# A bias moved into a matrix product, and two attention chunks contracted in halves

## What is computed

```python
x = layer_norm(ALPHA * x + mix, ln_mix_g[i], ln_mix_b[i])
x = layer_norm(ALPHA * x + swiglu(x, w_ffn_gate[i], w_ffn_up[i], w_ffn_down[i]), ln_ffn_g[i], ln_ffn_b[i])
gate = sigmoid(x @ w_ple_gate[i] + b_ple_gate[i])
x = x + (p[i] @ w_ple[i]) * gate          # then layer 1: qkv = x @ w_qkv + b_qkv, and attention
```

## Time and profile before

| | us |
|---|---|
| median of 3 runs | 1343.62 (1341.12 to 1346.0) |
| the profiled execution | 1346.43 |
| its span in the trace | 1344.5 |
| PE busy in the span | 1290.2 (96%) |
| DVE, ACT, POOL busy | 416.1, 648.8, 947.8 |
| mean granted clock of PE | 0.988 |

### The profile page before, as it was taken

One profiled execution on the slowest core, in us unless ns is written; L12 is line 12 of the kernel. 1 busy time (PEld: TensorE's weight loads), 2 busy tenths in 40 slices (PEclk: granted clock), 3 DMA queues, 4 the chain that ended last, 5 costly groups with the idle time before them and its releaser, 6 DMA issues.

```text
span 1344.5 us, 19614 instructions
## 1 busy us (share of the span) xinstructions
PE 1290.2 (96%) x8203; PEld 1154.0 (86%) x8203; DVE 416.1 (31%) x755; ACT 648.8 (48%) x841; POOL 947.8 (70%) x416
## 2 busy tenths in 40 slices
PE   6999999999999999999999999999988878999997
PEld 6988988878899988897899889998878658999885
DVE  5526325442222210045552131101153452101124
ACT  5673545755455553343444454435356544443442
POOL 6864246846969888756478778879976346786983
PEclk9999999999999999998999999999999998999999
DMA  8744134534656555635355756646637334663651
GB/s 276 210 128 126 48 110 132 182 108 127 220 152 199 183 195 195 188 93 159 104 173 188 245 169 183 175 138 211 224 113 265 108 94 129 172 193 119 234 189 47
DMA packets 117966, 218.60 MB, mean 163 GB/s; under 512 B 9415, under 2 KB 18934, under 8 KB 117750
## 3 DMA queue, kind: packets, MB, share of 16 engines
q1 hardware_dynamic: 113888, 209.92, 50.6%
q10 hardware_dynamic: 3990, 7.42, 1.6%
HBM read 216.27 MB, written 1.05 MB: 162 GB/s over the span
## 4 chain that ended last, share of the span: by engine, by line
PE 89%; DVE 7%; ACT 2%; issue 1%; DMA 1%; ACTq 0%; DVEq 0%
PE acc L1868 13%; PE acc L1870 13%; PE acc L1871 13%; PE acc L1861 12%; PE acc L1863 12%; PE acc L1862 12%; PE pm L1876 8%; PE acc L1819 1%; PE acc L1820 1%; PE acc L1821 1%; ACT pm L548 1%; PE pm L1785 1%; DMA ct<-in_consts 1%; DVE XTlo L1063 0%; DVE pm L1734 0%
## 5 line engine op out<-in xcount | busy, mean ns | idle before, releaser
L533 POOL TENSOR_TENSOR wlo<-raw,whi 128x1024 fp32r<-128x1024 f32 (+2 forms) x412 | 947.6, 2325 | 382.1 <-ACT whi L548 380.6
L548 ACT ACTIVATE whi<-raw 128x1024 fp32r<-128x1024 f32 (+2 forms) x412 | 412.4, 1019 | 354.1 <-PE acc L1871 154.2
L1868 PE MATMUL acc<-XThi,whi 128*128 128x256 f32 x1424 | 406.8, 286 | 5.5 <-issue 2.9
L1870 PE MATMUL acc<-XTlo,whi 128*128 128x256 f32 x1424 | 405.3, 285 | 0.0
L1871 PE MATMUL acc<-XThi,wlo 128*128 128x256 f32 x1424 | 405.3, 285 | 0.0
L1868 PEld LDWEIGHTS acc<-XThi,whi 128*128 128x128 f32 x1424 | 275.8, 194 | 6.9 <-issue 3.7
L1870 PEld LDWEIGHTS acc<-XTlo,whi 128*128 128x128 f32 x1424 | 275.8, 194 | 0.2
L1871 PEld LDWEIGHTS acc<-XThi,wlo 128*128 128x128 f32 x1424 | 275.7, 194 | 0.0
L1861 PE MATMUL acc<-whi,XThi 128*128 128x512 f32 (+3 forms) x320 | 125.8, 393 | 2.6 <-DVE xbcT L1492 1.6
L1863 PE MATMUL acc<-whi,XTlo 128*128 128x512 f32 (+3 forms) x320 | 121.5, 380 | 0.0
L1862 PE MATMUL acc<-wlo,XThi 128*128 128x512 f32 (+3 forms) x320 | 121.5, 380 | 0.0
(11 more groups left out here) (405 smaller groups left out, 1657.7 us busy)
## 6 DMA issues: line engine op xcount, KB each, us to landing
raw<-in_w_in SPq DMA_DIRECT2D x68, 512.0 KB, 3.7
raw<-in_w_ff SPq DMA_DIRECT2D x64, 512.0 KB, 3.7
raw<-in_w_in_mix SPq DMA_DIRECT2D x44, 512.0 KB, 3.6
raw<-in_w_down SPq DMA_DIRECT2D x44, 512.0 KB, 4.3
raw<-in_w_gate SPq DMA_DIRECT2D x40, 512.0 KB, 3.6
raw<-in_w_up SPq DMA_DIRECT2D x40, 512.0 KB, 3.7
raw<-in_w_branch SPq DMA_DIRECT2D x16, 512.0 KB, 3.5
raw<-in_w_out_mix SPq DMA_DIRECT2D x16, 512.0 KB, 3.5
```

Source lines behind the costliest of these rows:

```text
L533: nc.gpsimd.tensor_tensor(wlo[:, u % SPLIT, 0:nk, 0:width], raw[:, u % RAW, 0:nk, 0:width], whi[:, u % SPLIT, 0:nk, 0:width].bitcast(F32), ...
L548: return nc.scalar.activation(out_, in_, func, **k)
L1868: T.matmul(o, wh[:, fs], hi[:, k, :], start=opens and f % 2 == 0, stop=False, skip_group_check=True)
L1870: T.matmul(o, wh[:, fs], lo[:, k, :], start=False, stop=False, skip_group_check=True)
```

## The change

Two edits. First, `aq0` and `ak` are each cut into two chunks of 4 blocks: `aq0a`, `aka`, `aq0`, `ak` in this order, the first two `PARTIAL`, the last two `CONTINUED`. `aka` so stands ahead of PE's wait for `x_end` 2 and of groups 2 and 3 of the turn, and ACT's bound for its splits ahead of groups 2 and 3 becomes `begun("aka", 2) + AHEAD`. Second, each gate chunk opens with one more matmul for each tile of 128 tokens, before its first unit: `ones[0:1, :]` (one row, 128 columns) times `lnr[0:1, 4, ...]` (one row, 512 columns), both plain float32. The add of the bias on DVE is gone, and the sigmoid waits for PE.

```diff
-PARTIAL = ("mo0a", "mo1a", "ao0a", "ao1a", "ao0b", "ao1b")
-CONTINUED = ("mo0b", "mo1b", "ao0b", "ao1b", "ao0c", "ao1c")
+PARTIAL = ("aq0a", "aka", "mo0a", "mo1a", "ao0a", "ao1a", "ao0b", "ao1b")
+CONTINUED = ("aq0", "ak", "mo0b", "mo1b", "ao0b", "ao1b", "ao0c", "ao1c")
...
-            g.append(("aq0", "w_qkv", KD, 0, W, "F"))
-            g.append(("ak", "w_qkv", KD, D, AKV * AD, "F"))
+            for part, k0 in (("a", 0), ("", 4)):
+                g.append((f"aq0{part}", "w_qkv", 4, 0, W, "F", k0))
+                g.append((f"ak{part}", "w_qkv", 4, D, AKV * AD, "F", k0))
...
-                def sigmoid(part, view):
-                    act.wait_ge(S["g_x"], 2 * i + part + 1)
+                def sigmoid(done, view):
+                    act.wait_ge(*done)
                     fn(view, view, ACT.Sigmoid).then_inc(S["g_s"], 1)
...
-            high_halves(begun("aq0", 2) + AHEAD)
+            high_halves(begun("aka", 2) + AHEAD)
             turn("x6", XThi, first=2)
...
-                    V.tensor_tensor(gate, gate, lnr[:, 4, cols].unsqueeze(1).to_broadcast([P, n, W]), ALU.add)\
-                        .then_inc(S["g_x"], 1)
...
+            def biased(name):
+
+                if name[0:2] == "pg":
+                    n, c = chunks[name][0], int(name[4])
+                    for t in range(NT):
+                        T.matmul(acc[:, n % 2, t, :], ones[0:1, :], lnr[0:1, 4, c * W:(c + 1) * W], start=True,
+                                 stop=False)
...
-            product("aq0", XThi, XTlo, 0, 2, ready=turned("x6"))
+            product("aq0a", XThi[:, 0:4], XTlo[:, 0:4], ready=turned("x6"))
+            product("aka", XThi[:, 0:4], XTlo[:, 0:4])
             pe.wait_ge(S["x_end"], 2)
             turn("x6", X, first=2)
-            product("aq0", XThi, XTlo, 2, ready=turned("x6"))
-            product("ak", XThi, XTlo)
+            product("aq0", XThi[:, 4:8], XTlo[:, 4:8], ready=lambda j: turned("x6")(2 + j))
+            product("ak", XThi[:, 4:8], XTlo[:, 4:8])
```

More of the change, by code:

```diff
@@ L952, in feed_forward @@
                 turn_tile(("x5", "x8")[i], XThi, 1)
-                def sigmoid(part, view):
-                    act.wait_ge(S["g_x"], 2 * i + part + 1)
+                def sigmoid(done, view):
+                    act.wait_ge(*done)
                     fn(view, view, ACT.Sigmoid).then_inc(S["g_s"], 1)
                 high_halves(landed(f"pg{i}_0") + AHEAD)
-                sigmoid(0, accT(f"pg{i}_0"))
+                sigmoid((S["w_used"], landed(f"pg{i}_0")), accT(f"pg{i}_0"))
                 if i == 0:
@@ L962, in feed_forward @@
                     high_halves(landed("pg0_1") + AHEAD)
-                    sigmoid(1, accT("pg0_1"))
+                    sigmoid((S["w_used"], landed("pg0_1")), accT("pg0_1"))
                 else:
                     for t in range(NT):
-                        sigmoid(1 + t, accT("pg1_1")[:, t])
+                        sigmoid(((S["t_half"], 5), (S["w_used"], landed("pg1_1")))[t], accT("pg1_1")[:, t])
             feed_forward(0)
@@ L1818, in unit_T @@
                     wh, wl = whi[:, s, i, 0:width], wlo[:, s, i, 0:width]
-                    T.matmul(o, hi[:, k, tok], wh, start=k == 0 and name not in CONTINUED, stop=False)
+                    T.matmul(o, hi[:, k, tok], wh, start=k == 0 and name not in CONTINUED and name[0:2] != "pg",
+                             stop=False)
                     T.matmul(o, hi[:, k, tok], wl, start=False, stop=False)
@@ L1828, in tiles_apart @@
                     enter(name)
+                    biased(name)
                 for t in range(NT):
@@ L1843, in product @@
                 n, first, end, kt, width, mode, left = chunks[name]
-                begins, ends = name not in CONTINUED, name not in PARTIAL
+                begins, ends = name not in CONTINUED and name[0:2] != "pg", name not in PARTIAL
                 if start == 0:
                     enter(name)
+                    biased(name)
                 for u in range(first + start, end if stop is None else first + stop):
```

## The result

The changed kernel takes **1356.21 us** (median of 4 runs, 1353.7 to 1359.3), the kernel before in the same session 1344.71 (4 runs). The ratio is 1.0085, 95% interval 1.0062 to 1.0109. By these two ratios the change costs 8 to 11 us where 4.6 were forecast, and the time lies above the range.

The account below looks back on a forecast made before the run. PE was taken to bound the kernel, busy in 96% of the span and 89% of the chain. Bias products +6.86, end add −0.74 and halves −1.5 gave +4.6 us: 1343.62 to 1348.2 us, range 1344.5 to 1351.7.

Parts of the forecast that it names:

- the sum: Whole kernel: 6.86 − 0.74 − 1.5 = +4.6 us, with no term for the clock.
- the clock falls more often: Rival: the clock falls behind `pg0_0`'s wait too and stays low longer, +1.8 to +3.5 us, 1350.0 to 1351.7; chance 0.13.
- the 0.9 at which the prediction called itself wrong: Behind `pg0_0`: a granted clock below 0.9 was one of the stated signs of a wrong prediction.
- 64 rows are busy as long as 128: Earlier trace, 256-column products: 0.30 us each for both; time goes by columns, so 0.86 was taken for a one-row product.
- Own cost of the products, 6.86: PE at the four gate chunks: eight bias products of 0.86 us each, all 6.86 us on the path.
- Nothing covers them: `pg0_0` and `pg1_0`: the products would fit the 2.04 us wait, but the code puts them behind it.
- The add at the end, −0.74: End of the program, second tile of `pg1_1`: DVE's bias add goes, 0.74 us off the end.
- The halves, −1.5: PE's stall between `pg0_1` and the attention: 1.5 us won, bounds 1.2 and 1.7, about 1.1 us of stall left.
- Without the halves the shorter chain alone would have given 1.26: Same stall: ACT's chain starting 1.26 us earlier without the add; the two edits share the stall and don't add up.
- The base: Start of the forecast: the kernel before at its median of 1343.62 us, to which 4.6 was added.
- The clock falls less: Rival: the fall behind `pg1_0` may be absent when everything before it shifts, −1.8 us, giving 1346.4; chance 0.15.
- the products are nearly free: Rival: one-row products leave the array to neighbours; 1341.4 at no cost, 1343.2 at 0.23 us each; chance 0.06.

Follow-up runs that it names:

- The pairs with 128 rows: The changed kernel with the bias products contracted over 128 rows (1/128 times the bias row in every partition): 1349.52 us, ratio 1.0016.
- 32 rows: The changed kernel with the bias products contracted over 32 rows (1/32 times the bias): 1352.98 us, ratio 1.0073.
- the version with the products in the wait: The changed kernel with the one-row products of `pg0_0` and `pg1_0` issued ahead of PE's 2.04 us wait: 1349.09 us, ratio 1.0030.
- the trace with the products alone: The changed kernel without the halves, queries and keys in one piece each as before: 1355.5 us, ratio 1.0073.
- the halves alone: The changed kernel with the bias add back on DVE and no bias products: 1343.17 us, ratio 0.9968.
- filled waits: Changed kernel, bias products in 2.04 us waits: one-row `pg0_0`/`pg1_0` pairs 1349.09 us; only `pg0_1`/`pg1_1` as products, 128 rows 1340.93, one row 1342.48.
- One product at a time: The changed kernel with each gate chunk's two one-row products set apart by gate matmuls: 1359.09 us, ratio 1.0098.

## Why the prediction was wrong, point by point

**The step that failed is the clock: the sum put it at nothing, and only the rival "the clock falls more often" held it, in too small a place.** The rival had a chance of 0.13 and a price of +1.8 to +3.5. Its mechanism, "if 1.7 us of one-row products behind the wait don't count as work", fits what happened, and its sign came: the granted clock behind `pg0_0` was 0.65, below the 0.9 at which the prediction called itself wrong. It looked only at the two pairs behind a wait, since the earlier trace rows had a wait and a fall together. The fall needs no wait. In the kernel after it comes behind `pg0_1` and `pg1_1` too, where PE had been busy without a gap. Had the mechanism been priced at all four pairs, it would have been up to 4 × 1.7 = 6.8 us on the sum, giving 1355.0, with 1353.01 and 1356.21 measured in the two sessions. The pairs with 128 rows, at the same places and with the same columns, show that it is the rows addressed that make the difference: 4.5 us of clock in the means of the runs.

**The trace of before already had falls without a wait.** The prediction looked at the clock only around the gate. From 175.23 us PE makes 24 plain float32 matmuls with 64 stationary columns, and from 608.12 to 613.4 us matmuls with 16 moving columns. It is busy all the time, and the clock falls, in the second place while these matmuls still run (they grow from 0.26 to 0.36 us). The first view is the timeline, the second the granted clock around the first place:

```profile
175.23 4.18 PE L1876 MATMUL pm<-dn 128*64 128x128 f32 x24
...
612.95 0.26 PE L1863 MATMUL acc<-whi,XTlo 128*128 128x16 f32 x1
613.06 0.27 PE L1861 MATMUL acc<-whi,XThi 128*128 128x16 f32 x1
613.18 0.36 PE L1862 MATMUL acc<-wlo,XThi 128*128 128x16 f32 x1
```

```profile
177.00:179.50 2.50, 2.50 (x14) 1.60 (x14) 0.05 (x1) 0.00 (x0) 2.50 (x2) 1.00 0.77 214
179.50:183.20 3.70, 3.70 (x19) 3.70 (x20) 2.20 (x5) 0.00 (x0) 1.34 (x1) 0.54 0.72 234
```

The matmuls at 613 address all 128 rows, so few rows are not the only work behind which the clock falls. In eleven of the twelve traces it falls while these matmuls run, between 610.5 and 613.5 us, in the twelfth right behind them. No experiment changed these products, so what in them matters is open.

The Trainium skill, "TensorE: Matmul & The Clock Gate", section "What's actually happening", ties the clock to how busy PE has been. Here PE is busy by every row of the profile and the clock falls nonetheless, so busy time is not the measure of it; the section doesn't say what is.

**The rival got too small a chance for a reason that was in view.** The prediction took from the earlier trace rows that 64 rows are busy as long as 128, and carried it over from duration to everything else. Duration is all that these rows show; of the clock they say nothing.

**Own cost of the products, 6.86.** Right for 128 rows: 7.0 in the trace, 4.3 and 4.6 net of the gains in the rest of the runs, against a sum of 4.6. For one row the term was mis-sized by 0.9 us: the ledger leaves 7.8 without the clock. Behind a wait a pair costs 1.8, near the 1.72 forecast, but where PE runs without a gap 2.0 to 2.2, against about 1.8 for 128 rows; there 32 rows cost as much as one. In the means of the runs one row stands 1 to 2 us above 128 rows, which the three digits of the clock blur. The Trainium skill, "TensorE: Matmul & The Clock Gate", section "Why this matters for your kernels", says that a single product of 32 rows takes as long as one of 128. At the full clock its records do (587 and 592 ns), the stream around it, where PE runs without a gap, doesn't (2.1 to 2.2 against 1.8 us a pair). "Nothing covers them" was right as well; the version with the products in the wait shows by 8.68 against 8.66 us that the cover was there to be had.

**The add at the end, −0.74.** Right: 0.6 less from the last matmul to the end.

**The halves, −1.5.** Right in size for what both edits do together (28.61 to 27.09), and right in what is late next: the transposes, then 0.97 us of wait where 1.1 were forecast. The split between the edits was wrong. "Without the halves the shorter chain alone would have given 1.26" put 0.3 us on the halves beside the bias product; the trace with the products alone reaches 27.02, so they add nothing to it there. Up to 0.9 us of the 2.56 before was a slow DMA issue of ACT in that one execution, the one for `bv` taking 1.48 us where ten other traces have 0.49 to 0.62 (one more has 1.68). It doesn't explain the gain away: over 12 runs the halves alone take 2.2 us off the rest of the span.

**The base.** The forecast started from 1343.62; beside the changed kernel the one before stood at 1344.71, which is 1.1 of the 8.0 us missed. The own cost is about 0.9 of them and the clock 3.5 (mean of all ten runs of the changed kernel, against 15.4 before) to 4.9 (those four). The rest, 1.1 to 2.5, is within what medians of four runs scatter. In the two profiled executions the account closes: of the 13.0 us 4.6 were forecast, 6.8 are the clock at the gate, 0.9 the own cost, 0.1 the end, and 0.6 stand between the first score and `pg1_0`, where nothing was changed.

**The clock falls less** and **the products are nearly free** did not come about. The fall behind `pg1_0` is indeed a matter of the execution: the kernels with halves alone, with 128 rows and with filled waits don't show it.

## What to carry to other kernels

A bias as a one-row product is not the price of one matmul: it may bring the clock down behind it, though PE is never idle. If an addition is to be put on PE, let it contract over all partitions (a stationary matrix with one live row, or with 1/128 everywhere, was enough), and put it into a wait that PE has anyway: that took the changed kernel from 0.85% slower to 0.27% faster. The halves alone are 0.32% faster, so the bias products, placed well, cost nothing, and a gain from them is not shown in the runs. Before an add is moved to the engine that sets the time, look at which of the instances stand on the path: here two of the four chunks, and the other two paid for nothing.

## What the runs showed that was not expected

- The granted clock falls to 1.2 GHz behind products that address few rows, behind those of one row also while PE is busy without a gap: behind 12 of 18 pairs of one row, 2 of 4 of 32 rows (both behind a wait), 0 of 10 of 128 rows, also where 127 of the 128 stationary rows hold zeros (all pairs in the profiled executions, those in filled waits among them). With no wait just ahead it is 5 of 8 for one row, 0 of 2 for 32 rows, 0 of 4 for 128. A stretch of 3.4 us at the lower clock costs 1.7 us.
- It also falls while PE is busy with matmuls of all rows and 16 columns, in 11 of 12 traces (610.5 to 613.5 us).
- A pair of plain float32 products of 512 columns costs a stream without a gap about 1.8 us with 128 rows and 2.0 to 2.2 us with 1 or 32; directly behind a wait all of them cost 1.7 to 1.8.
- One product at a time was no cure: 1359.09 us against 1353.01 in pairs in the same session. What decides whether one such product is followed by a fall stays open.
- A wait of 2.04 us that is filled with 128-row products costs nothing (8.65 us with them and without) and no fall followed it (0 of 2); filled with one-row products, 1 of 4 had one (`pg0_0` of the kernel with two pairs in waits).
